# Hyena's transformed data by way of device memory in three of its eight steps

## The reference

```python
def long_conv(u, hf, bias):
    seqlen = u.shape[1]
    uf = jnp.fft.rfft(u, n=2 * seqlen, axis=1)
    y = jnp.fft.irfft(uf * hf[None], n=2 * seqlen, axis=1)[:, :seqlen]
    return y + u * bias

def hyena(p, lp, rows, row_len):
    ...
    hf = hyena_filters(seqlen, lp)
    z = x1 * long_conv(v, hf[:, 0], bias[0])
    z = x2 * long_conv(z, hf[:, 1], bias[1])
    return z * jax.nn.silu(p['z_b'].astype(f32))
```

## Time and profile before

| | us |
|---|---|
| median of 3 runs (lowest, highest) | 4163.44 (4159.42, 4169.43) |
| the profiled execution | 4165.86 |
| its span, first to last instruction | 4164.1 |
| PE busy | 4033.0 (97%) |
| DVE busy | 2773.3 (67%) |
| POOL busy | 1769.2 (42%) |
| ACT busy | 1215.4 (29%) |

### The profile page before, as it was taken

The page is one execution under the profiler, slowest core; times in us unless marked ns, Lnnn a source line. Parts: engine busy times, 40 slices in busy tenths (PEclk is TensorE's granted clock), DMA queues, the critical chain, the costliest instruction groups (busy, mean ns, idle before and its releaser), DMA issues. The chain is left out here.

```text
span 4164.1 us, 75281 instructions
## 1 busy us (share of the span) xinstructions
PE 4033.0 (97%) x29523; PEld 2528.0 (61%) x29523; DVE 2773.3 (67%) x4294; ACT 1215.4 (29%) x2587; POOL 1769.2 (42%) x1498
## 2 busy tenths in 40 slices
PE   6999999999999999999998999989999998999998
PEld 4455544444444444444445999976666665888887
DVE  5667855542447786887644777757776777668766
ACT  5112111111211211112113666655555654010000
POOL 1322233332233334333335666635454545455653
PEclk8999999999999999999999999999999999999999
DMA  8233222223242442324336898748676878746542
GB/s 284 80 86 105 85 89 82 81 91 117 88 156 82 127 117 78 111 81 121 121 106 187 261 260 245 230 124 231 213 232 215 244 229 265 253 162 212 197 151 98
DMA packets 480697, 655.76 MB, mean 157 GB/s; under 512 B 82897, under 2 KB 373657, under 8 KB 470493
## 3 DMA queue, kind: packets, MB, share of 16 engines
q1 hardware_dynamic: 431898, 518.82, 40.2%
q0 software_dynamic: 26448, 104.86, 7.9%
q10 hardware_dynamic: 22002, 27.27, 2.0%
HBM read 438.04 MB, written 212.81 MB: 156 GB/s over the span
## 5 line engine op out<-in xcount | busy, mean ns | idle before, releaser
L1546 PE MATMUL proj_b<-shared_S,proj_tw 128*128 128x512 f32 x1920 | 848.1, 593 | 0.0
L1546 PEld LDWEIGHTS proj_b<-shared_S,proj_tw 128*128 128x128 f32 x1920 | 360.4, 190 | 432.6 <-issue 431.9
L1546 PE MATMUL proj_b<-shared_A,shared_wt 128*128 128x512 f32 x1280 | 576.9, 593 | 6.6 <-PEq L161 6.6
L874 POOL TENSOR_TENSOR proj_tw<-shared_wt 128x512 f32<-128x512 f32 x80 | 115.9, 1449 | 881.1 <-PE proj_b L1546 821.7
L1546 PEld LDWEIGHTS proj_b<-shared_A,shared_wt 128*128 128x128 f32 x1280 | 243.7, 191 | 310.6 <-issue 310.2
L1546 PE MATMUL proj_b<-shared_A,proj_tw 128*128 128x512 f32 x640 | 289.6, 595 | 4.2 <-DVE proj_u L1188 4.2
L1546 PE MATMUL proj_b<-shared_S,shared_wt 128*128 128x512 f32 x640 | 290.1, 596 | 0.0
L1091 ACT ACTIVATE proj_v<-proj_b 128x512 f32<-128x512 f32 x80 | 47.8, 597 | 662.3 <-PE proj_b L1546 662.3
L1183 DVE TENSOR_TENSOR proj_u<-proj_b,proj_u 128x512 f32<-128x512 f32 x80 | 55.2, 691 | 275.0 <-PE proj_b L1546 274.9
L1546 PEld LDWEIGHTS proj_b<-shared_A,proj_tw 128*128 128x128 f32 x640 | 122.0, 191 | 159.0 <-issue 150.4
L888 POOL TENSOR_TENSOR proj_tw<-shared_wt,proj_tw 128x512 f32<-128x512 f32 x80 | 117.1, 1463 | 212.6 <-PE proj_b L1546 212.5
(11 more groups left out here) (417 smaller groups left out, 8979.4 us busy)
## 6 DMA issues: line engine op xcount, KB each, us to landing
shared_wt<-in_w_in_dram POOLq DMA_DIRECT2D x80, 1024.0 KB, 6.0
scratch_bounce_f<-tail_first SPq DMA_DIRECT2D x128, 256.0 KB, 4.5
bridge_region<-scratch_bounce_f SPq DMA_DIRECT2D x32, 1024.0 KB, 7.5
scratch_bounce_i<-fft_yi SPq DMA_DIRECT2D x64, 512.0 KB, 3.5
fft_second<-scratch_bounce_i SPq DMA_DIRECT2D x32, 1024.0 KB, 8.6
scratch_hy<-shared_hA SPq DMA_DIRECT2D x48, 512.0 KB, 2.6
delta_ring_kq<-scratch_KQ SPq DMA_DIRECT2D x88, 256.0 KB, 4.3
delta_ring_nv<-scratch_NV SPq DMA_DIRECT2D x84, 256.0 KB, 5.0
```

The source lines that it names most:

```text
L874: pool.tensor_tensor(T3, w[:, hi, second], w[:, lo, second], ALU.subtract).then_inc(combined, 1)
L1546: last = pe.matmul(bank[:, :], weights[:, k, :], aa[operand][:, k, :], start=(k == 0), stop=(k == KH - 1))
```

## The change

Steps 2, 4 and 6 (`dealt`) regroup the data by way of device memory, as the filters are regrouped in all steps. Four things follow from it.

First, in these steps ACT and DVE copy a D bank as it is, one contiguous row, into `first`; SP writes the four blocks to a new buffer `bounce_d` (1 MB each), waits for all four, and reads pairs of four regrouped rows back (`data_fetch`, 1 MB each) into the first half of `first`. Each read back serves two pairs h; the third and fourth overwrite the first and second, so they wait for X of pairs 1 and 3. The matrix product of D has its two operands exchanged, so that frequencies come out on the partitions. Second, the transposes T of these steps and their evictions are gone, and X reads the regrouped rows in `first`. Third, the exchange stands in another order: one block of O, all of D, the other blocks of O, Z. Fourth, SP's list has new entries. The function `filters_first` and the branch on it have no effect, since `dealt` holds for no odd step and not for step 0.

```diff
+        dealt = lambda t: t % 2 == 0 and t > 0
...
+        def exchange_order(t):
+
+            out = [("O", c) for c in range(4)] if t else []
+            data = [("D", c) for c in range(4)] if t < STEPS else []
+            results = [("Z", 0)] if t and t % 2 == 0 else []
+            if t == STEPS:
+                return out[0:2] + [("W", 1)] + out[2:4] + results
+            if t % 2 == 0 and dealt(t):
+                return out[0:1] + data + out[1:4] + results
+            return out[0:2] + data[0:1] + out[2:3] + data[1:2] + out[3:4] + data[2:3] + results + data[3:4]
...
+                def data_deal(t):
+                    for c in range(4):
+                        read(sp, "D", t, 4 * c + 2)
+                        read(sp, "D", t, 4 * c + 3)
+                        sp.dma_start(T["bounce_d"][t % 2, :, 4 * c:4 * c + 4, :, :], ya[:, 4 * c:4 * c + 4, :, :]).then_inc(yc_out, 16)
+                    sp.wait_ge(yc_out, 64 * (dealt_before(t) + 1))
+
+                def data_fetch(t, c):
+                    if c >= 2:
+                        ready(sp, "X", t, 4 * c - 5)
+                    sp.dma_start(dealt_pair(c).rearrange("p (g c) -> p g c", c=CB), by_four(T["bounce_d"][t % 2], c)).then_inc(yd_in[c % 2], 16)
...
                     filter_read(t, 0)
                     filter_read(t, 1)
+                    if dealt(t) and o == 0:
+                        data_deal(t)
+                        data_fetch(t, 0)
+                        data_fetch(t, 1)
...
                     for h in range(PAIR):
+                        if dealt(t) and h in (0, 2):
+                            data_fetch(t, h // 2 + 2)
                         read(sp, "I", t, 2 * h + 1)
...
+                        if dealt(t):
+                            dst, src = first[:, 2 * CB * n:2 * CB * (n + 1)], bank("D", t, n)[:, :]
...
+                            if dealt(t):
+                                last = pe.matmul(b[:, half].rearrange("p (b c) -> p b c", b=2), fa[:, n, r, :], u[:, block_of(t), :, n, :], start=True, stop=True)
...
                 def data_spectrum(t, h):
-                    read(pe, "T", t, 2 * h)
-                    read(pe, "T", t, 2 * h + 1)
-                    tiles("X", t, h, mats["fb"], lambda j: yd[:, j, :])
+                    if dealt(t):
+                        c = h // 2
+                        pe.wait_ge(yd_in[c % 2], 16 * (2 * dealt_before(t) + c // 2 + 1))
...
                         for h in range(PAIR):
-                            data_spectrum(t, h)
-                            if 0 < h < PAIR - 1:
+                            if not filters_first(t, h):
+                                data_spectrum(t, h)
+                            if 0 < h < PAIR - 1 and not dealt(t):
                                 turn(t, h + 1)
```

More of the change, by code:

```diff
@@ L2155, in hyena @@
         xs, pre, pim = (xs0, xs1), (pre0, pre1), (pim0, pim1)
+        QK = 4 * CB
+        dealt = lambda t: t % 2 == 0 and t > 0
+        dealt_before = lambda t: len([x for x in range(t) if dealt(x)])
+        dealt_pair = lambda c: first[:, 2 * QK * (c % 2):2 * QK * (c % 2 + 1)]
+        dealt_four = lambda h: dealt_pair(h // 2)[:, QK * (h % 2):QK * (h % 2 + 1)].rearrange("p (i x) -> p i x", i=2)
         yt = ga[:, :, :, :].rearrange("p b n c -> p b (n c)")
@@ L2229, in hyena @@
         f_in, f_written = [kit.sem("f_in0"), kit.sem("f_in1")], kit.sem("f_written")
+        yc_out, yd_in = kit.sem("yc_out"), [kit.sem(f"yd_in{i}") for i in range(2)]
         i_written, o_in = [kit.sem("i_written0"), kit.sem("i_written1")], [kit.sem(f"o_in{c}") for c in range(4)]
@@ L2446, in _ @@
                 for t in range(STEPS + 1):
-                    if t < STEPS:
-                        for c in range(3):
-                            empty_data(t, c)
                     if t == STEPS:
@@ L2455, in _ @@
                         first_turned((2, 3))
-                    if t and t % 2 == 0:
-                        empty_out(t // 2 - 1)
+                    for x, c in exchange_order(t):
+                        if x == "D":
+                            empty_data(t, c)
+                        if x == "Z":
+                            empty_out(t // 2 - 1)
                     if t < STEPS:
-                        empty_data(t, 3)
-                        empty_turn(t, 0)
+                        if not dealt(t):
+                            empty_turn(t, 0)
                         ready(act, "S", t, 0)
@@ L2743, in data @@
                         b = take("D", t, n)
-                        for h in range(2):
-                            last = pe.matmul(b[:, h * CB:(h + 1) * CB], u[:, block_of(t), h, n, :], fa[:, n, :, :].rearrange("p r k -> p (r k)"), start=True, stop=True)
+                        for r in range(2):
+                            half = slice(r * CB, (r + 1) * CB)
+                            if dealt(t):
+                                last = pe.matmul(b[:, half].rearrange("p (b c) -> p b c", b=2), fa[:, n, r, :], u[:, block_of(t), :, n, :], start=True, stop=True)
+                            else:
+                                last = pe.matmul(b[:, half], u[:, block_of(t), r, n, :], fa[:, n, :, :].rearrange("p r k -> p (r k)"), start=True, stop=True)
                         last.then_inc(filled, 1)
```

107 lines of the change are left out of this document (65 added, 42 removed).

## The result

| | before | after |
|---|---|---|
| median of 4 runs each (lowest, highest), us | 4166.43 (4159.42, 4170.36) | 4187.77 (4181.22, 4190.86) |
| the profiled execution, its span, us | 4165.86, 4164.1 | 4181.22, 4179.4 |

The account below looks back on a forecast made before the run. It took PE, 97% busy, with a nearly late DMA chain on SyncE's queue, as the bound; steps 4, 6 and 2 add 5.0 + 7.7 + 6.3 = 19 us to 4163.4, giving 4182 us, range 4159 to 4196.

Parts of the forecast that it names:

- D and Z: Exchange on PE: D stalls 0.1 us, Z waits 1.5 us for DVE and starts 5.0 us later in step 4.
- Deals and reads 0, 1: Deals take 10.6 us behind the filter reads; first two reads back land at 3185.9 and 3188.9; X(0) waits up to 0.9.
- y and gates: SP's queue: y issued at 3185.4, stored at 3194.2 behind the second read back; gates go out 7.4 us later.
- X(4) and R(4): Loop in step 4: PE waits about 12 us at X(4) and again at R(4), which comes 6.7 us late.
- The second wait: PE at R(4) waits for the filter read, landing at 3215.4, behind the gates and the third read back.
- The loop: Period 3.5 us; R(4) to R(7) 12.0 us with a slow-clock stretch; steps 4, 6, 2 end 5.0, 7.7, 6.3 us later.
- the first inverse write: Named as queued behind in the loop; its landing frees ACT's buffer for I(2); no size given.
- The first rival: Reads back all arrive before PE wants them: 5 to 6 us less a step, 17 in all, 4146 us; chance 0.13.

Follow-up runs that it names:

- late-y kernel: Changed kernel with y kept in the free half of `first`, stored in two halves behind the loop's inverse writes 4 and 5: 4165.43 us, ratio 0.9994 to before.
- the trio: Changed kernel with all four reads back ahead of the y store (4198.23 us); third and fourth on ScalarE's queue instead (4197.75); their filter reads there too (4203.84).
- the last runs: Gates split between SyncE and GpSimd on the late-y kernel (4173.55 us) and the kernel before (4164.08); late-y kernel with half the gates behind the third read back (4167.93).
- the control: Kernel before the change, with the gates of steps 2, 4 and 6 issued half by SyncE's and half by GpSimd's queue: 4164.08 us, ratio 0.9993.

## Why the prediction was right

The sign, the size and the mechanism came out as forecast; one part of the sum came out near by luck. By the steps, in step 4 and from its start:

- **D and Z.** D runs behind the first O without a stall (0.1 forecast). Z waits 1.51 us for DVE, as read from the earlier trace rows, and starts at 29.7 us (29.3 forecast).
- **Deals and reads 0, 1.** Down at 30.1 us (29.0), but not on the way that the sum took. It let the deals run on behind the filter reads; in the trace the last is issued only at 18.6 us, when the last D bank has been copied, and lands 11.4 us later. That the end fits so well is partly luck. X(0) waits 1.44 us (up to 0.9), and at 35.7 it is 1.3 us later than before, a little beyond the 1 us allowed.
- **y and gates.** y issued at 34.6 us (34.2), but landed 10.7 us later, where the sum had 8.8 and the earlier trace rows give 6.4 for it undisturbed. Read 1, behind which the sum put y's data, landed 1.6 us later than forecast, and y 6.0 us behind it (5.3). So the gates are 9.7 us later than before, not 7.4. This is the term that was mis-sized.
- **X(4) and R(4).** One long wait at X(4), 12.4 to 13.7 us (12). R(4) 8.6 us late (6.7): the 2.3 us of the gates less 0.4. The second wait, for the filter read at R(4), is there too, but short and seen only on the weight loads: 1.48 us, ended by the read that landed at 3223.5. So it is this read that times R(4), as the sum had it.
- **The loop.** A period of 3.4 us (3.5), X(2) at 3198.69 to X(3) at 3202.07; R(4) to R(7) 12.4 us (12.0), with the lower clock of 0.50 in the hole. Step 4 ends 7.0 us later (5.0), step 6 7.9 (7.7), step 2 8.05 (6.3): 23.0 for 19. In the profiled run the rest of the program was 8 us shorter, as single runs of either kernel differ by. The medians' 21 and the steps' 23 agree well enough with 19.

The late-y kernel shows the cause: it keeps the new order and the round trip, and changes only where y lies and is stored, so that the gates don't wait for it and its bytes come later; and the loss is gone. What the prediction had only half is what lies behind it. It put the sum on read 2 and the filter read and named the first inverse write in a clause; the trio shows that this write alone holds the loop as long, and in the changed kernel itself it ended ACT's wait only 1.3 us behind X(4)'s. And it priced a place in the queue, not the bytes: in the stretch of 20 us from 3171 to 3191 the engines' share was 0.42 before and is 0.87 in the kernel after (3177.5 to 3197.5), so moving a transfer ahead mostly moves the wait. That bytes set the rest of the time is argued from these shares and the last runs, not shown: the control gained in its steps from a second queue. The first rival's gain of 17 us came with none of the orders tried.

On the queue the Trainium skill's rule that was cited (DMA: Bandwidth & Descriptors, "Queues, rings and completion order") agrees: read 2, the inverse write and the filter read, issued at 3207.73, 3208.21 and 3210.38, landed in that order, and none overtook the gates; the overtaking that the rule allows isn't seen. Its HBM figure of about 358 GB/s, the share of a core when both of a pair stream, was no limit here, with one core running: the deals ran at 431 GB/s. A rule that the prediction did not use is in the Trainium skill's SBUF — State Buffer: a transfer into the first 64 partitions reaches half the ports, with an asymptote of about 218 GB/s, and one into the last 64 the other half ("Door 1: The DMA port swizzle"); two at once, one to each half, measured only 6% more than one ("Can I just issue two DMAs to hit both halves?"). The traces fit: the gates, two transfers to each half, ran at 210 to 227 GB/s, and at 231 to 237 from two queues. That the ports are the cause no run here shows; the gates are also read from every other row of their source.

What stays open: whether one gate transfer over all 128 partitions would be faster, which was not tried; why the order alone cost 14 us by the times and 6.7 by its trace; and what lengthens the VectorE instruction in step 7.

## What to carry to other kernels

An operation taken off the busiest engine is worth only what the transfers that replace it leave of it: look at the stage's DMA share and at what is queued behind the last transfer that has to wait for something. Where several transfers stand behind one late one, release that one; lifting the others past it one by one only changes the name of the wait. And when the wait moves without shrinking, count bytes and rates, not places in the queue.

## What was not expected of the hardware

- While the gates moved, the 16 DMA engines showed a busy share of 1.0 at 210 to 227 GB/s, and the same share at 431 GB/s for whole rows. The share alone does not tell the two apart.
- Issuing itself grew: one filter read held SP for 0.51 us before, 4.65 after and 5.11 in the late-y kernel, with the gates in flight in all three and read 2 in the queue ahead of it in the last two. SP's next issue waits for that too. What makes it grow was not tried. The row of 7.57 us for the four deals is another thing: each issue takes 0.3 to 1.1 us, and between them SP waits for the copies of D. The last is issued here:

```profile
3176.15 0.32 SPq L2321 DMA_DIRECT2D scratch_bounce_d<-tail_first  x1
```
